# A decoder step on one core: the first-layer values of every fourth expert block made beside the gate tables, and the state copies in four places

## The reference, cut to what matters

```python
q = (xi @ wq).reshape(PEER_TOKEN_BLOCK, PEER_HEADS, 2, PEER_DKEY // 2)
s = jnp.einsum('nhcd,ckd->nhck', q, subkeys)
sv, si = lax.top_k(s, K)
...
g = jax.nn.softmax(top_s, axis=-1)
hpre = jnp.einsum('nd,nhkd->nhk', xi, u_tab[eid])
a = (jax.nn.gelu(hpre, approximate=False) * g).astype(xi.dtype)
return jnp.einsum('nhk,nhkd->nd', a, v_tab[eid])
...
kc = jnp.concatenate([state_k_win, kd_s], axis=1)
vc = jnp.concatenate([state_v_win, vd_s], axis=1)
```

## Time and profile before

| what | value |
|---|---|
| median of 3 runs | 2648.16 us (2646.22 to 2648.57) |
| the profiled execution's own time | 2648.93 us |
| its span | 2647.1 us |
| PE, PE weight loads, DVE, ACT, POOL busy in the span | 87%, 74%, 61%, 35%, 14% |
| granted clock of PE, mean | 0.917 |
| chain that ended last | PE 68%, DVE 10%, DMA 5% |
| gate stage, from its first instruction to the barrier | about 1110.7 to 1420.3 us |
| expert stage | about 1420.3 to 2606 us |

### The profile page before, as it was taken

One profiled execution on the slowest core, in us unless ns is written; L12 is line 12 of the kernel. 1 busy time (PEld: TensorE's weight loads), 2 busy tenths in 40 slices (PEclk: granted clock), 3 DMA queues, 4 the chain that ended last, 5 costly groups with the idle time before them and its releaser, 6 DMA issues.

```text
span 2647.1 us, 38437 instructions
## 1 busy us (share of the span) xinstructions
PE 2289.9 (87%) x13177; PEld 1955.8 (74%) x13177; DVE 1610.1 (61%) x3159; ACT 928.9 (35%) x1417; POOL 359.4 (14%) x370
## 2 busy tenths in 40 slices
PE   7997879998997989504376999999999999999994
PEld 7996656666664469503376999999999999999993
DVE  3433322343434347799994667777677776777767
ACT  3225533444445122102263333333333333333331
POOL 0000000000000000100000223222232222322230
PEclk9998879899988989856687999999999999999997
DMA  3220026667665111299965888888787887878873
GB/s 121 91 73 33 1 91 200 201 207 225 198 201 190 64 48 49 80 323 339 364 263 201 278 274 283 275 281 278 272 284 275 282 278 273 285 273 282 278 273 105
DMA packets 214837, 555.47 MB, mean 210 GB/s; under 512 B 16993, under 2 KB 87202, under 8 KB 212066
## 3 DMA queue, kind: packets, MB, share of 16 engines
q1 hardware_dynamic: 165730, 315.16, 36.3%
q0 software_dynamic: 49024, 239.23, 25.4%
HBM read 521.95 MB, written 98.83 MB: 235 GB/s over the span
## 4 chain that ended last, share of the span: by engine, by line
PE 68%; DVE 10%; DMA 5%; SPq 2%; ACT 2%; issue 1%; POOLq 0%; DVEq 0%; ACTq 0%; POOL 0%
PE psum L1913 20%; PE psum L1925 19%; PE psum L1523 4%; PE psum L1903 4%; DMA gates_dram<-gate_table 3%; PE psum L978 3%; PE psum L1386 3%; PE psum L1050 2%; PE psum L1032 2%; DVE gate_table L1726 2%; PE psum L968 2%; PE psum L1000 2%; DMA sample<-in_cache_v_sb_dram 2%; DVE gate_table L1723 1%; PE psum L1766 1%
## 5 line engine op out<-in xcount | busy, mean ns | idle before, releaser
L1913 PE MATMUL psum<-h_parts,expert_parts 128*128 128x384 f32 x3072 | 592.9, 341 | 4.2 <-DVE expert_parts L2013 4.2
L1925 PE MATMUL psum<-expert_parts 128*128 128x512 f32 x2304 | 557.2, 395 | 0.0
L1913 PEld LDWEIGHTS psum<-h_parts,expert_parts 128*128 128x128 f32 x3072 | 537.7, 189 | 14.6 <-DVE expert_parts L2013 4.8
L1925 PEld LDWEIGHTS psum<-expert_parts 128*128 128x128 f32 x2304 | 423.3, 188 | 83.5
L2013 DVE TENSOR_TENSOR expert_parts<-psum,expert_parts 128x512 fp32r<-128x512 f32 x256 | 177.1, 692 | 293.2 <-ACT expert_parts L1955 293.2
L1961 ACT ACTIVATE expert_parts<-peer 128x1024 fp32r<-128x1024 f32 x128 | 135.8, 1061 | 365.9 <-PE psum L1925 365.9
L1955 ACT ACTIVATE expert_parts<-psum 128x512 fp32r<-128x512 f32 x256 | 153.1, 598 | 200.5 <-PE psum L1903 200.5
L2053 DVE SCALAR_TENSOR_TENSOR kept<-experts,kept 128x1024 f32<-128x1024 f32 x160 | 204.7, 1280 | 3.9 <-DVE kept L2043 2.8
L1305 DVE TENSOR_TENSOR sample_parts<-sample,sample_parts 128x512 fp32r<-128x512 f32 x128 | 85.2, 690 | 158.0 <-ACT sample_parts L1158 158.0
L394 PE MATMUL psum<-projection_parts 128*128 128x256 f32 (+1 forms) x1440 | 173.7, 282 | 3.8 <-DVE projection_parts L500 3.8
L1883 POOL DMA_INDIRECT experts<-in_peer_u_dram,kept x96 | 113.0, 1178 | 468.5 <-DVE experts L2037 345.4
(11 more groups left out here) (271 smaller groups left out, 2993.7 us busy)
## 6 DMA issues: line engine op xcount, KB each, us to landing
peer<-in_peer_u_dram SPq DMA_DIRECT2D x128, 512.0 KB, 5.6
peer<-in_peer_v_dram SPq DMA_DIRECT2D x128, 512.0 KB, 3.7
sample<-in_cache_k_sb_dram SPq DMA_DIRECT2D x128, 256.0 KB, 3.1
sample<-in_cache_v_sb_dram SPq DMA_DIRECT2D x128, 256.0 KB, 3.0
out_dram<-in_state_k_win_dram POOLq DMA_DIRECT2D x8, 4088.0 KB, 104.9
out_dram<-in_state_v_win_dram POOLq DMA_DIRECT2D x8, 4088.0 KB, 118.2
gates_dram<-gate_table SPq DMA_DIRECT2D x12, 2048.0 KB, 8.4
experts<-gates_dram SPq DMA_DIRECT2D x32, 768.0 KB, 6.0
```

The source lines that it names most:

```text
L1913: last = pe.matmul(bank(6)[:, 0:ND], lhsT=u_t[s][:, a, k, :], rhs=h1_r[:, b, k, 0:ND], start=(k == 0 and n == 0), stop=(k == KD - 1 and n ...
L1925: last = pe.matmul(bank(2 * t + half), lhsT=weight[s][:, a, t * P:(t + 1) * P], rhs=v_r[s][:, b, half * 512:(half + 1) * 512], start=(firs ...
```

## The change

Of four blocks (a set, `SET = 4`) the last one, `x = 4e + 3`, is taken out of the expert stage's first layer. For these 32 blocks (e = 0 to 31) the gate stage loads the rows of u, PE transposes them (two halves, bank 7) and multiplies them with `h1_f`, a new unsplit fp32 copy of `h1` for the 384 tokens, in 8 fp32 matmuls of 384 columns (bank 6); ACT copies the transposes, applies Gelu, and SP stores 128x384 values in `gelu_dram`. `gate_schedule` says where: blocks 0 to 11 ahead of the first `turn`, 12 to 16 ahead of the second, 17 to 19 in chunks 1 to 3 (a half after each half of the chunk), 20 to 24 ahead of the third `turn`, 25 to 31 in chunks 4 to 10. ACT's five `Exp` of the gates stand behind fixed blocks (`EXP_AFTER`). The banks of the table products go in threes instead of fours.

In the expert stage `is_full(k)` leaves out `hidden` and `turn_u` for the fourth block; its values are loaded from `gelu_dram` into `gelu_e` and multiplied with the gates. The counters of u go by full blocks (`full_of`). DVE's dots and additions of a set are at other blocks: additions (0, 1), (2), (3), (4) and dots (0), (1, 2), (3), (4).

The 16 state copies are issued as 7 in the stick-breaking stage (after its `counts_in` load), 4 in the dilated stage, 3 in the output projection and 2 in the query projection. That stage's products have 384 and 256 columns instead of 320 and 320.

```diff
+        MOVES = (7, 4, 3, 2)
+        EXP_AFTER = {1: 0, 5: 1, 10: 2, 15: 3, 22: 4}
+        BLOCK_OF = {1: 17, 2: 18, 3: 19, 4: 25, 5: 26, 6: 27, 7: 28, 8: 29, 9: 30, 10: 31}
+        FIRST_OF = ((0, 12), (12, 17), (20, 25))
...
+            def hidden_early(e, half):
+                pe.wait_ge(sem("early_copied"), 2 * e + half + 1)
+                if half == 0 and e >= 1:
+                    pe.wait_ge(sem("early_gelu"), e)
+                for k in range(4 * half, 4 * half + 4):
+                    last = pe.matmul(bank(6)[:, 0:ND], lhsT=early_t[e % 2][:, k, :], rhs=h1_f[:, k, :],
+                                     start=(k == 0), stop=(k == KD - 1))
+                if half == 1:
+                    last.then_inc(sem("early_hidden"), 1)
...
+            def block(e):
+                if e >= 1:
+                    gelu_early(e - 1)
+                copy_early(e + 1, 0)
+                copy_early(e + 1, 1)
+                exponents(e)
...
             def load(turn):
                 for k in range(2 * SET):
                     x = 2 * SET * turn + k
+                    if k % SET == 0:
+                        if not (isinstance(turn, int) and turn == 0 and k == 0):
+                            sp.wait_ge(sem("weight_low"), x - 2)
+                        sp.dma_start(gelu_e[k // SET], gelu_dram[bass.ds(2 * turn + k // SET, 1)].rearrange("o p n -> (o p) n"))\
+                            .then_inc(sem(f"gelu_in_{k // SET}"), 16)
                     if not (isinstance(turn, int) and turn == 0 and k < 2):
-                        sp.wait_ge(sem("u_turned"), 2 * x + 2)
-                        sp.dma_start(u_sb[k % 2], peer_u[bass.ds(x * P, P), :]).then_inc(sem(f"u_in_{k % 2}"), 16)
+                        if is_full(k):
+                            j = full_of(k)
+                            sp.wait_ge(sem("u_turned"), 2 * (FULL * turn + j) + 2)
+                            sp.dma_start(u_sb[j % 2], peer_u[bass.ds(x * P, P), :]).then_inc(sem(f"u_in_{j % 2}"), 16)
                         sp.wait_ge(sem("v_low"), x + 1)
                         sp.dma_start(v_sb[k % 2], peer_v[bass.ds(x * P, P), :]).then_inc(sem(f"v_in_{k % 2}"), 16)
...
-                    for half in range(2):
-                        hidden(x, s, half)
-                        if not is_last(turn, k):
-                            turn_u(x + 1, 1 - s, SET * turn + (k + 1) // 2, half)
+                    if is_full(k):
+                        j = full_of(k)
+                        f = FULL * turn + j
+                        for half in range(2):
+                            hidden(f, j % 2, half)
+                            if not is_last(turn, k):
+                                turn_u(f + 1, 1 - j % 2, FULL // 2 * turn + (j + 1) // 2, half)
```

More of the change, by code:

```diff
@@ L1698, in _ @@
                         sp.dma_start(h1_s[g * NS:(g + 1) * NS, :], x_nat[0:NS, NT - 1, :]).then_inc(sem("sample_rows_in"), 16)
-                over_chunks(sp, t, store)
-            sp.wait_ge(sem("table_out_0"), 16 * (NCHUNK // 2 + 1))
-            sp.wait_ge(sem("table_out_1"), 16 * (NCHUNK // 2 + 1))
+                if e is not None:
+                    block(e)
+                sp.wait_ge(sem("table_copied"), 4 * c + 7)
+                sp.dma_start(gates_dram[c], table[c % 2].rearrange("p i n -> p (i n)")).then_inc(sem(f"table_out_{c % 2}"), 16)
+            for e in range(3):
+                load(e)
+            gate_schedule(turn, block, chunk)
+            store(SETS - 1)
+            for e in range(2):
+                sp.wait_ge(sem(f"early_out_{e}"), 16 * (SETS // 2))
+                sp.wait_ge(sem(f"table_out_{e}"), 16 * (NCHUNK // 2 + 1))
         @part("pool")
         def _(pool):
-            for b in range(DB):
-                for to, frm in ((k_win_sample, state_k_win), (v_win_sample, state_v_win)):
-                    pool.dma_start(to[b].rearrange("w h d -> (w h d)")[0:(WIN - DT) * DH],
-                                   frm[b].rearrange("w h d -> (w h d)")[DT * DH:WIN * DH]).then_inc(sem("window_moved"), 16)
             pool.wait_ge(sem("ijg_ready"), NT)
@@ L1758, in turn, with turn_early @@
                 last.then_inc(sem("ijg_turn"), 1)
-            def spread(c, s, i):
+            def turn_early(e, half):
+                if e == SETS:
+                    return
+                if half == 0:
+                    pe.wait_ge(sem(f"early_in_{e % 2}"), 16 * (e // 2) + 16)
+                pe.wait_ge(sem("early_copied"), 2 * e + half)
+                for k in range(4):
+                    last = pe.transpose(bank(7)[:, k * P:(k + 1) * P], early_u[e % 2][:, 4 * half + k, :], ident)
+                last.then_inc(sem("early_turned"), 1)
@@ L1771, in _ @@
-            for t in range(NTD + 1):
-                if t < NTD:
-                    turn(t)
-                if t >= 1:
-                    pe.wait_ge(sem("ijg_turned"), min(t + 1, NTD))
-                    over_chunks(pe, t - 1, spread)
+                    for q in range(2 * half, 2 * half + 2):
+                        r = 4 * c + q
+                        pe.wait_ge(sem("table_copied"), r + 1)
+                        for n in range(QUARTER):
+                            at = q % 2 * QUARTER + n
+                            last = pe.matmul(bank(2 * (r % 3) + n // 4)[:, n % 4 * NK:(n % 4 + 1) * NK],
+                                             lhsT=hot_j[half][:, at, :], rhs=hot_i[half][:, at, :], start=True, stop=True)
+                        last.then_inc(sem("table_ready"), 1)
@@ L1778, in _ @@
+                    if e is not None:
+                        block_half(e, half)
+            turn_early(0, 0)
+            turn_early(0, 1)
+            gate_schedule(turn, block, chunk)
         @part("act")
         def _(act):
-            act.drain().then_inc(sem("table_copied"), 4)
+            act.drain().then_inc(sem("table_copied"), 3)
             act.drain().then_inc(sem("table_out_0"), 16)
             act.drain().then_inc(sem("table_out_1"), 16)
-            def copy(c, s, i):
-                act.wait_ge(sem(f"table_out_{s}"), 16 * i + 16)
-                for q in range(4):
-                    act.wait_ge(sem("table_ready"), 4 * c + q + 5)
-                    act.activation(table[s][:, :, 8 * q:8 * q + 8].rearrange("p i n -> p n i"),
-                                   bank(2 * q, 2).rearrange("p (n i) -> p n i", n=8), ACT.Copy).then_inc(sem("table_copied"), 1)
@@ new lines, in block, with turn, chunk @@
+            def block(e):
+                if e >= 1:
+                    gelu_early(e - 1)
+                copy_early(e + 1, 0)
+                copy_early(e + 1, 1)
+                exponents(e)
+            def turn(t):
+                act.wait_ge(sem("ijg_turn"), t + 1)
+                act.activation(ijg_t[:, :, t * P:(t + 1) * P], bank(0)[:, 0:3 * P].rearrange("p (x n) -> p x n", x=3), ACT.Copy)\
+                    .then_inc(sem("ijg_turned"), 1)
+            def chunk(c, e):
+                act.wait_ge(sem(f"table_out_{c % 2}"), 16 * (c // 2) + 16)
+                if e is not None:
+                    gelu_early(e - 1)
+                for half in range(2):
+                    for q in range(2 * half, 2 * half + 2):
+                        r = 4 * c + q
+                        act.wait_ge(sem("table_ready"), r + 5)
+                        act.activation(table[c % 2][:, :, QUARTER * q:QUARTER * (q + 1)].rearrange("p i n -> p n i"),
+                                       bank(2 * (r % 3), 2).rearrange("p (n i) -> p n i", n=QUARTER), ACT.Copy)\
+                            .then_inc(sem("table_copied"), 1)
+                    if e is not None:
+                        copy_early(e + 1, half)
@@ L1804, in build @@
+            copy_early(0, 0)
+            copy_early(0, 1)
+            gate_schedule(turn, block, chunk)
+            gelu_early(SETS - 1)
         for engine in programs:
@@ L1831, in build, with is_full, full_of @@
         weight = [take_r(2 * ND).rearrange("p (s n) -> p s n", s=2) for _ in range(2)]
+        gelu_e = [take(ND) for _ in range(2)]
+        FULL = 2 * (SET - 1)
+        def is_full(k):
+            return k % SET != SET - 1
+        def full_of(k):
+            return k // SET * (SET - 1) + k % SET
         gates_g = gates_dram.rearrange("c p (g n) -> p c g n", g=SETS)
```

197 lines of the change are left out of this document (133 added, 64 removed).

## The result

The changed kernel takes 2690.29 us (median of four runs, 2687.3 to 2696.91) against 2648.36 us before (four runs beside it): ratio 1.0159, 95% interval 1.0135 to 1.0183. It is slower by 1.6%, inside the predicted 2618 to 2724 us and 8 us above the forecast of 2682. The profiled execution took 2687.3 us, its span 2685.5, 38.4 more than before.

What follows compares the result with a forecast made beforehand. TensorE (PE) was taken to bound the expert stage and DVE the gate stage, where PE becomes the bound. Expert stage +18, gate stage +16 and copies 0 gave +34: 2682 us, range 2618 to 2724 us.

Steps and rivals of the forecast that it cites:

- The expert stage, +18 forecast: Expert stage: 163 us of TensorE work removed, but a late u load and lower clock make a set 37.5 us; +18 us.
- the queue: Expert stage, SP: the next set's first u stands behind the fourth block's v load, issued 9.6 us after the second block's start.
- the landing: Expert stage: the next set's first u load lands 5.4 us after its issue.
- the stall: Expert stage, third block: TensorE waits 3.8 us for u in each set.
- the clock: Expert stage: behind each pause TensorE's clock falls for a while, costing 2.0 us a set.
- Rival A: Expert stage: u lands in 4.0 us and the clock holds, a set of 33.8 us; -80 us, 2568 us; chance 0.14.
- B: Expert stage: something frees SP earlier, u is not late, TensorE bound at 31.68 us a set; 2501 us; chance 0.06.
- C: Gate stage: TensorE's waits for ACT let its clock fall to half for a sixth of its work; +48 us, 2730; chance 0.07.
- The gate stage, +16 forecast: Gate stage: the early blocks make TensorE the bound there; +15 us, put at +16 with the odd handover.
- The copies, 0 forecast with 0 to +6: Stages ahead of the gate stage: the moved copies run in idle DMA time or hidden behind TensorE's work; 0, at most +6 us.
- rival D: Output projection: the norm weights hold it up; +6 us, 2688 us; chance 0.05.
- the 2689 us: Gate stage: the forecast sum if five table switches on TensorE's way each also cost the skill page's drain, 6.9 us more.

Runs made afterwards that it cites:

- the filled pause: The changed kernel with 28 extra transposes of the identity on TensorE in each set's third block, ahead of its wait for the late u load: 2648.49 us, ratio 0.9999.
- Moving one small load: The changed kernel with the 192 KB load of Gelu values issued behind the u and v loads of the set's first block, not ahead of u: 2648.24 us, ratio 0.9998.
- the kernel with u first: The changed kernel with the next set's first u load issued ahead of the fourth block's v load instead of behind it: 2518.87 us, ratio 0.9509.
- the kernel with the copies alone: The kernel before with only the state copies moved, 7, 4, 3 and 2 at the changed kernel's four places: 2665.01 us, ratio 1.0057.

## Why the prediction was right

**The expert stage, +18 forecast, +7.5 measured.** The mechanism is the one foretold, in every step: the queue (u issued at 9.6 us after the second block's start by the sum, 9.71 in the set shown), the landing (5.4 against 5.10), the stall (3.8 against 3.96 us a set), the 31 times, and no new wait at `v_low`, since TensorE never waits ahead of `add_up`. The term that was mis-sized is the clock: 2.0 us taken between two rows of the gate stage, 1.4 by the filled pause. A set is 37.28 instead of 37.5 us, 31 x 0.22 = 7 us of the 10.5 missing; the other 3.5 must lie at the ends of the stage, which I did not follow. The granted clock of the stage is 0.96, not near 0.9 as the prediction's own sign had it.

**Rival A** would have needed a landing in 4.0 us. The median of the u loads after is 5.2 us in the stretch from 1990 to 2100 us, and none of the 31 was in time. Moving one small load already goes a third of the way to A (42 of the 122 us between 2690 and A's 2568): ratio 0.9998, no change from before.

**Rivals B and C.** B, the u load not late, is what the kernel with u first makes: 2519 us, which is B's 2501 and nearly the 19.4 us of the copies. In the changed kernel the queue's order stood against it, as foretold. C, a low clock in the gate stage, didn't come: the granted clock is 0.98 from 1130 to 1442 us, and TensorE's waits for the Gelu of the block before are 10.1 us in all.

**The gate stage, +16 forecast, +11.5 measured.** The time line held: from the stage's start to the first table product 127.8 us by the sum, 126.0 measured; to the end of the last one 316 against 312.4. The two pieces under the sum are larger and of opposite sign than I had put them: the early blocks +18.8, the copies' leaving -7.3 instead of some -5, both from the kernel with the copies alone. That they come near the forecast together is in part chance.

**The copies, 0 forecast with 0 to +6, +19.4 measured.** This is the step that failed. Three things were wrong in it. First, the text let seven and four copies end at 359 us as one row of work and looked only at the sample stage's loads from 373 us. It did not ask about the barrier at 304 between them, where each engine is drained, and which opened only when POOL's seventh copy had landed: +6.1. The sign it had named, the barrier ahead of the sample stage standing where it did, failed too: that stage's first load comes at 378.15 instead of 373.65 us. Second, the norm weights were to come some 20 us after the barrier and DVE's delay of up to 6 us was to be covered by TensorE's second tile; the last of them came 30.5 us after it, and the stage grew by 10.0. That is rival D, with more than its +6. Third, "two take 26 us beside a load wanted 60 us later" looked at the wrong load. The query weights wanted at once took 27.06 us: +3.3.

**The sum.** +7.5 + 11.5 + 19.4 = 38.4 us of span, against +34. It came out within 8 us because the expert stage was put 10.5 too high and the gate stage 4.5, and the copies 19.4 too low: that closeness is luck. The direction didn't hang on it: without the copies' 19.4 the other two stages still lose 19.0, since the expert stage, which was to be rid of 163 us of work, gave nothing.

**The two pages.** ScalarE's table loads stand back to back with the Exp in the trace after (rows of ACT's timeline):

```profile
1149.95 1.28 ACT L1903 ACT_TABLE_LOAD   x1
1151.25 0.31 ACT L1903 ACTIVATE kept<-kept 128x128 f32<-128x128 f32 x1
1151.58 1.28 ACT L1898 ACT_TABLE_LOAD   x1
1152.87 0.49 ACT L1898 ACTIVATE kept<-psum 128x384 f32<-128x384 f32 x1
```

Nothing lies between them (1149.95 + 1.28 + 0.31 ends within 0.04 us of the next load's start), and TensorE's pause at such a switch is 1.18 us, 0.95 more than its usual 0.23:

```profile
1146.05 2.82 PE L1846 MATMUL psum<-h_whole,gate_table 128*128 128x384 f32 x8 [0.23 <-ACT kept L1898]
...
1153.50 2.82 PE L1846 MATMUL psum<-h_whole,gate_table 128*128 128x384 f32 x8 [1.18 <-ACT kept L1898]
```

The Trainium skill ("ScalarE: Activation LUTs", What ACT_TABLE_LOAD costs) adds a drain of about 1380 ns each time. The trace disagrees with the page here; the 2689 us that followed are near the result for other reasons.

The norm weights are two loads of 512 KB. The first landed after 4.1 us. The second, issued 0.4 us later, took 30.1 us, where it took 5.3 in the kernel before. These are the DMA queues of the kernel after from 882 to 908 us, then those of the kernel with all copies in the gate stage from 1120 to 1300 us (packets, MB, share of the engines; POOL's copies are on q0, SP's transfers on q1):

```profile
q0 software_dynamic: 160, 8.37, 90.7%
q1 hardware_dynamic: 160, 0.53, 8.3%
...
q0 software_dynamic: 1120, 58.48, 94.9%
q1 hardware_dynamic: 1122, 3.09, 5.4%
```

Both queues moved the same number of packets, but a packet of the copies holds 52 KB and one of SP's about 3. The Trainium skill ("DMA: Bandwidth & Descriptors", Queues, rings and completion order) has a DMA engine go round between queues packet by packet. The trace agrees with that in these two stretches. Wrong were the equal packets of the prediction, from which the 7 us were worked out: turns were shared evenly, bytes 16 to 1. Beside the query weights the counts are not equal (128 packets of copies to 1201 of 1 KB from 976 to 1000 us), and what makes a turn there stays open.

## What to carry to other kernels

When work is taken out of a loop, follow each load that is now wanted earlier back to its place on the queue that issues it. Here two lines of order decided between +1.6% and -4.9%, in a place where the same order had been worth nothing. In this kernel a copy in the background was free only where it was over at the next barrier that drains its issuer, and where no load wanted soon was issued beside it. A long wait of one engine says nothing before it is known whether another engine's work covers it: moving the Exp that VectorE waited 14 us for gave back 1.8 us at most.

## What the runs showed of the hardware that was not expected

- **The barrier held until the copies issued by POOL, which is drained there, had landed.** Seven copies: TensorE idle 6.54 us at the barrier, which opened 0.4 us after the seventh had landed; six: 0.51 us; none, in the kernel before: 0.51 us. Other queues than POOL's weren't tried.
- **Sixteen copies of 4.19 MB can hold up other loads for most of their own time.** Loads of 512 KB kept TensorE waiting up to 41.6 us, 183.6 us in all, beside 205 us of copies. The queues took equal numbers of packets, of 52 KB against about 3 KB.
- **A pause of about 4 us often costs twice.** Behind the pause of 4.30 us that ends at 2079.74 TensorE's granted clock is 0.50, its lower level (1.2 GHz), from 2080 to 2083 us and 0.99 in the next 3 us; behind the one of 3.49 us that ends at 2006.47 it is 1.00. With transposes in the pause it stays at 1.00, and a set is 1.4 us shorter though nothing useful was added.
